# Third attention of a two-block transformer: key, value and query blocks in two halves, heads attended between blocks

## What is computed

```python
def second_block(...):
    ...
    for layer in range(DEPTH):
        mod = c_act @ ada_w[layer] + ada_b[layer]
        sh1, sc1, g1, sh2, sc2, g2 = jnp.split(mod, 6, axis=-1)
        hn = modulate_2(rms_norm_2(h, norm1_g[layer]), sh1, sc1)
        y = recurrent_mixer(hn, ...) if layer < N_A_LAYERS else chunk_attention(hn, ..., k_pad, v_pad)
        h = h + g1[:, None, :] * y
        hn = modulate_2(rms_norm_2(h, norm2_g[layer]), sh2, sc2)
        h = h + g2[:, None, :] * sqrelu_mlp(hn, mlp_w1[layer], mlp_w2[layer])
        if layer == N_A_LAYERS - 1:
            k_pad, v_pad = shared_kv(h, c_act, kv_norm_g, kv_ada_w, kv_ada_b, kv_w, k_norm_g)

def shared_kv(h, c_act, ...):
    ...
    hn = modulate_2(rms_norm_2(h, kv_norm_g), shift, scale)
    k, v = jnp.split(hn @ kv_w, 2, axis=-1)
    k = rms_norm_2(k.reshape(bsz, s, N_HEADS, HEAD_DIM), k_norm_g)      # 16 heads of 64

def chunk_attention(hn, w_q, q_norm_g, rel_bias, w_o, k_pad, v_pad):
    ...
    q = rms_norm_2((hn @ w_q).reshape(bsz, s, N_HEADS, HEAD_DIM), q_norm_g)
    sc = jnp.einsum("bqhd,bkhd->bhqk", qc, kc) * scale + bias           # relative bias, masked
    p = jax.nn.softmax(sc, axis=-1)
    return jnp.einsum("bhqk,bkhd->bqhd", p, vc) @ w_o
```

## Time and profile before

| | us |
|---|---|
| three runs of the kernel before | 1739.34, 1744.42, 1745.04 |
| their median | 1744.42 |
| the profiled execution's own time | 1744.36 |
| its span in the profile | 1742.6 |
| PE busy | 1666.6 (96%) |
| DVE busy | 1285.7 (74%) |
| ACT busy | 826.7 (47%) |
| POOL busy | 243.3 (14%) |
| granted clock of TensorE, mean | 0.99 of full speed |

### The profile page before, as it was taken

One profiled execution on the slowest core, in us unless ns is written; L12 is line 12 of the kernel. 1 busy time (PEld: TensorE's weight loads), 2 busy tenths in 40 slices (PEclk: granted clock), 3 DMA queues, 4 the chain that ended last, 5 costly groups with the idle time before them and its releaser, 6 DMA issues.

```text
span 1742.6 us, 28904 instructions
## 1 busy us (share of the span) xinstructions
PE 1666.6 (96%) x11946; PEld 1487.3 (85%) x11946; DVE 1285.7 (74%) x1777; ACT 826.7 (47%) x1196; POOL 243.3 (14%) x199
## 2 busy tenths in 40 slices
PE   6999989999999999999999999969999999899999
PEld 3897667788788876986999999959999999699999
DVE  4777863887988878857578777797998878657453
ACT  3433762543224333636554546575636444555362
POOL 0323001011001111440310121013000220030000
PEclk9999999999999999999999999989999999999999
DMA  8744002233565458320347566634998956037542
GB/s 304 276 159 169 2 1 97 97 145 115 187 241 203 175 202 311 122 73 2 122 151 272 204 202 244 217 123 172 357 364 323 335 213 240 27 125 287 187 176 73
DMA packets 46578, 317.87 MB, mean 182 GB/s; under 512 B 5232, under 2 KB 6256, under 8 KB 12272
## 3 DMA queue, kind: packets, MB, share of 16 engines
q1 hardware_dynamic: 45936, 312.68, 49.2%
q0 software_dynamic: 512, 3.35, 0.5%
HBM read 314.96 MB, written 1.05 MB: 181 GB/s over the span
## 4 chain that ended last, share of the span: by engine, by line
PE 81%; DVE 11%; ACT 3%; issue 3%; POOL 2%; DMA 1%; DVEq 0%; ACTq 0%
PE PM L1629 22%; PE PM L1630 22%; PE PM L1631 22%; PE PM L1904 2%; DVE wlo L1030 2%; PE PX L1940 1%; DVE acc L1064 1%; PE PX L1602 1%; PE PX L1813 1%; PE PO L1966 1%; PE PX L1870 1%; PE PO L1955 1%; DVE Hlo L1527 1%; PE PM L1713 1%; PE PM L1715 1%
## 5 line engine op out<-in xcount | busy, mean ns | idle before, releaser
L1629 PE MATMUL PM<-Hhi,whi 128*128 128x256 f32 (+1 forms) x1686 | 525.9, 312 | 8.6 <-DVE Hlo L1441 3.0
L1630 PE MATMUL PM<-Hlo,whi 128*128 128x256 f32 (+1 forms) x1686 | 522.1, 310 | 0.0
L1631 PE MATMUL PM<-Hhi,wlo 128*128 128x256 f32 (+1 forms) x1686 | 521.9, 310 | 0.0
L1030 DVE TENSOR_TENSOR wlo<-raw,whi 128x2048 fp32r<-128x2048 f32 (+2 forms) x199 | 438.0, 2201 | 96.7 <-ACT whi L721 96.1
L721 ACT ACTIVATE whi<-raw 128x2048 fp32r<-128x2048 f32 (+3 forms) x204 | 365.5, 1791 | 150.8 <-PE PM L1631 95.1
L1629 PEld LDWEIGHTS PM<-Hhi,whi 128*128 128x128 f32 x1686 | 322.2, 191 | 33.4 <-issue 9.7
L1631 PEld LDWEIGHTS PM<-Hhi,wlo 128*128 128x128 f32 x1686 | 322.4, 191 | 16.5
L1630 PEld LDWEIGHTS PM<-Hlo,whi 128*128 128x128 f32 x1686 | 322.4, 191 | 15.8
L1629 PE MATMUL PM<-Ghi,whi 128*128 128x256 f32 (+1 forms) x864 | 265.2, 307 | 1.7 <-DVE X L1211 1.6
L1631 PE MATMUL PM<-Ghi,wlo 128*128 128x256 f32 (+1 forms) x864 | 263.2, 305 | 0.0
L1630 PE MATMUL PM<-Glo,whi 128*128 128x256 f32 (+1 forms) x864 | 263.2, 305 | 0.0
(11 more groups left out here) (226 smaller groups left out, 2244.8 us busy)
## 6 DMA issues: line engine op xcount, KB each, us to landing
raw<-in_ada SPq DMA_DIRECT2D x104, 1024.0 KB, 4.9
raw<-in_wm SPq DMA_DIRECT2D x93, 1024.0 KB, 5.0
raw<-in_wl SPq DMA_DIRECT2D x68, 1024.0 KB, 4.9
raw<-in_wl SPq DMA_DIRECT2D x32, 704.0 KB, 4.2
raw<-in_wm SPq DMA_DIRECT2D x5, 768.0 KB, 4.4
raw<-in_wm SPq DMA_DIRECT2D x4, 704.0 KB, 4.1
X<-in_x SPq DMA_DIRECT2D x1, 2048.0 KB, 12.0
bias<-in_bias POOLq DMA_DIRECT2D x1, 2048.0 KB, 11.1
```

Source lines behind the costliest of these rows:

```text
L1030: dve.tensor_tensor(wslot(wlo, i, usize(u)), slot_raw(n, usize(u)), wslot(whi, i, usize(u)).bitcast(F32), ALU.subtract)\
L1629: pe.matmul(out, st_hi, mv_hi, start=first, stop=False)
L1630: pe.matmul(out, st_hi, mv_lo, start=False, stop=False)
L1631: return pe.matmul(out, st_lo, mv_hi, start=False, stop=last)
```

## The change

It has three parts.

**Start.** The squares of chunks 1 to 6 of the first norm are added on DVE (counter sqadd_dve), and PE sums two instead of eight. The first ada pieces to be loaded are those of direct half 2, then w0, then the others; the order of the direct work on PE, DVE and ACT follows. The warm matmuls are 8 and 2 in place of 10 and 8, the 8 ahead of a wait. ACT makes split_hi(0) before lam's exponential, and its first Hhi waits for ada_first_done(0), which DVE now does behind its second xr.

**KV and M1.** The order of units becomes k0 k1 v4 v5 q0 q1, k2 k3 v6 v7 q2 q3 (156 to 167). The step of norm 7 goes; its pieces are worked in steps 156 to 159 (query_part, query_hi, query_lo) into the second half of Hhi and Hlo. The attention's steps are ordered by head group first; steps 0 to 4 are spread over units 162 to 166 and later, the rest comes in m_late between parts of the first two out units (168, 169), whose products over k 0 to 3 need the first head group alone. Units 156 to 169 share the two halves of one PM bank, the scores have the other; so each score group waits for the add (sadd) of the group before. The evacuation's squares go to rsum, and keep_busy stands before turns 5 to 7 alone.

**Ada pieces.** The three pieces of units 160 to 162 go to 83, 86 and 89. Since pieces are numbered in order, every piece behind those takes an earlier place: rows(15) follows unit 93, its last piece (63) being at 92; the last rows (24) follow 153 and not 163.

The weights are laid out in the new order. The core of the diff:

```diff
-    for n in range(8):
-        add("k" if n < 4 else "v", "KV", n, KD, 256, 256, nt=2)
-    for n in range(4):
-        add("q", "M1", n, KD, 256, 256, nt=2)
+    for half in range(2):
+        for kind, at_ in (("k", 0), ("v", 4), ("q", 0)):
+            for n in range(at_ + 2 * half, at_ + 2 * half + 2):
+                add(kind, "M1" if kind == "q" else "KV", n, KD, 256, 256, nt=2)
...
-WARM_TURN = {("L1", "cq"): 3, ("L1", "bq0"): 3, ("M1", "q"): 4}
+WARM_TURN = {("L1", "cq"): 3, ("L1", "bq0"): 3}
...
+EARLY = {KV0 + 6 + n: n for n in range(5)}
...
-                if key == ("q", 0):
-                    prog.append(("norm", 7, "M1", 256))
...
-              *range(160, 163), *range(173, 177)]:
+              83, 86, 89, *range(173, 177)]:
...
-DIRECT_ORDER = [0, 2, 1, 3, 4, 5, 6, 7]
+DIRECT_ORDER = [2, 0, 3, 1, 4, 5, 6, 7]
...
-    order = [("ada", a) for a in ADA_FIRST[:4]] + [("w", 0)] + [("ada", a) for a in ADA_FIRST[4:]] + [("w", 1)]
+    order = [("ada", a) for a in ADA_FIRST[:2]] + [("w", 0)] + [("ada", a) for a in ADA_FIRST[2:]] + [("w", 1)]
...
         def pm(i, a, n):
-            return PM[:, i % 2, a:a + n]
+            if KV0 <= i < OUT0 + 2:
+                return PM[:, 0, i % 2 * 512 + a:i % 2 * 512 + a + n]
...
             root(0, 512)
+            split_hi(0)
             act.wait_ge(*at("prep", "lam"))
             act.activation(view(lamt[:, :], "p (l c) -> p l c", l=2)[:, :, 2:4], view(lamt[:, :], "p (l c) -> p l c", l=2)[:, :, 0:2],
                            ACT.Exp).then_inc(*tick("prepa", "lam"))
-            split_hi(0)
...
+                        if n == 0 and s == 0:
+                            act.wait_ge(*at("aux_dve", ("ada", ("first", 0))))
...
+                    n = EARLY.get(i)
+                    if n == 3:
+                        m_spread_copy(1)
+                    if n:
+                        m_turn_copy(n - 1)
                     evac(u)
+                    if KV0 <= i < KV0 + 4:
+                        query_hi(2 * (i - KV0))
+                        query_hi(2 * (i - KV0) + 1)
+                    if n == 4:
+                        m_out_hi(1)
+                    elif n is not None:
+                        m_exps(n)
...
+            def m_late(last):
+
+                m_max(4)
+                qk_copy(last)
+                m_max(5)
+                m_turn_copy(4)
+                m_max(6)
+                m_reciprocal(5)
+                m_turn_copy(5)
+                m_max(7)
+                m_turn_copy(6)
+                m_product(5)
+                m_reciprocal(7)
+                m_turn_copy(7)
+                m_out_lo(5)
+                m_product(7)
+                m_out_lo(7)
+
...
-            arow_copy(0)
+            for k in range(1, added(0)):
+                if k > 1:
+                    dve.wait_ge(*at("sqadd_dve", (0, k - 1)))
+                dve.wait_ge(*at("sq", (0, k)))
+                dve.tensor_tensor(sqslot(0, 0, 512), sqslot(0, 0, 512), sqslot(0, k, 512), ALU.add).then_inc(*tick("sqadd_dve", (0, k)))
             arow_copy(2)
+            ada_first_done(2)
...
+                        if n == 0 and s == 1:
+                            arow_copy(0)
+                            ada_first_done(0)
...
+                    if n:
+                        m_turn_copy(n - 1)
+                    if n == 3:
+                        m_product(1)
                     evac(u)
...
+            def m_scores(n):
+
+                x = MS[n]
+                t, nk, j = x["t"], x["nk"], x["h0"] // 4
+                pe.wait_ge(*at("aux_dve", ("qkT", unit_of("k", "KV", j), 1)))
+                pe.wait_ge(*at("aux_dve", ("qkT", unit_of("q", "M1", j), 1)))
+                if n:
+                    pe.wait_ge(*at("sadd", ("M1", n - 1)))
+                for e, h in enumerate(x["heads"]):
...
+            def m_late():
+
+                out_part(UNITS[OUT0], range(4))
+                m_scores(4)
+                out_part(UNITS[OUT0 + 1], range(4))
+                transposes(UNITS[OUT0 - 1])
+                m_scores(5)
+                m_turn(4, False)
+                m_scores(6)
+                m_turn(5, True)
+                m_values(4)
+                m_scores(7)
+                m_spread(5)
+                m_turn(6, True)
+                m_values(5)
+                m_turn(7, True)
+                m_values(6)
+                m_spread(7)
+                m_values(7)
...
             pe.wait_ge(*at("cstdma", 0))
+            warm(("first", 0), 8)
             pe.wait_ge(*at("prep", "sel"))
-            warm(("first", 0), 10)
-            for k in range(3):
-                sumsq(0, k, 512)
+            direct_part(2, 0)
+            direct_part(2, 1)
+            sumsq(0, 0, 512)
+            sumsq(0, 7, 512)
+            direct_columns(2)
             direct_part(0, 0)
-            for k in range(3, 5):
-                sumsq(0, k, 512)
             direct_part(0, 1)
-            for k in range(5, 7):
-                sumsq(0, k, 512)
-            direct_part(2, 0)
-            sumsq(0, 7, 512)
-            direct_part(2, 1)
             direct_columns(0)
-            direct_columns(2)
-            warm(("first", 1), 8)
+            warm(("first", 1), 2)
             late = []
...
+                    n = EARLY.get(i, 9)
+                    if n < 4:
+                        m_scores(n)
+                    if n == 3:
+                        m_spread(1)
                     for v in turned_at(i):
                         transposes(v)
+                    if 1 <= n <= 4:
+                        m_turn(n - 1, False)
+                    if 2 <= n <= 4:
+                        m_values(n - 2)
```

More of the change, by code:

```diff
@@ L154, in first_of, with unit_of @@
     return next(u["i"] for u in UNITS if u["kind"] == kind and u["st"] == st)
+def unit_of(kind, st, idx):
+    return next(u["i"] for u in UNITS if u["kind"] == kind and u["st"] == st and u["idx"] == idx)
+KV0 = first_of("k", "KV")
+OUT0 = first_of("out", "M1")
+EARLY = {KV0 + 6 + n: n for n in range(5)}
 def norm_pieces(n, W):
@@ new lines, in m_spread_copy, with m_turn_copy @@
+            def m_spread_copy(m):
+                key = ("R", "M1", MS[m]["grp"])
+                g = groups["M1", MS[m]["grp"]]
+                before = [q for q, v in groups.items() if v == g - 2 and q[0] == "M1"]
+                if before:
+                    act.wait_ge(*at("otlo", before[0]))
+                act.wait_ge(*at("aux", key))
+                act.activation(tslot(g % 2), aux(key), ACT.Copy).then_inc(*tick("aux_act", key))
+            def m_turn_copy(m):
+                key = ("T", "M1", m, 0)
+                if t_copier(MS[m], 0) != "aux_act":
+                    return
+                act.wait_ge(*at("aux", key))
+                if pt_before(m) is not None:
+                    act.wait_ge(*at("pv", ("M1", pt_before(m))))
+                act.activation(MT[m][:, 0:512], aux(key), ACT.Copy).then_inc(*tick("aux_act", key))
@@ L975, in _ @@
                 elif step[0] == "attn":
[L976 to L977 removed]
+                    if step[1] == "M1":
+                        m_late()
+                    else:
+                        attn(step[1])
                 elif step[0] == "lsplit":
@@ L1206, in residual @@
                 cs = chunks_of(u)
-                each = 256 if u["kind"] == "lpart" else 512
+                each = 256 if u["kind"] == "lpart" or OUT0 <= i < OUT0 + 2 else 512
                 for m, c in enumerate(cs):
@@ new lines, in m_turn @@
+            def m_turn(m, busy):
+                x = MS[m]
+                nc_ = x["nk"] // 128
+                pieces = [(e, c) for e in range(4) for c in range(nc_)]
+                per = len(pieces) // t_banks(x)
+                for b in range(t_banks(x)):
+                    key = ("T", "M1", m, b)
+                    dst = take(key)
+                    if busy and b == 0:
+                        keep_busy(dst)
+                    if b == 0:
+                        pe.wait_ge(*at("p", ("M1", m)))
+                    for c in range(per):
+                        ins = pe.transpose(dst[:, c * 128:c * 128 + 128], MP[m][:, m_piece(m, *pieces[b * per + c])], ident)
+                    ins.then_inc(*tick("aux", key))
@@ new lines, in m_spread @@
+            def m_spread(m):
+                key = ("R", "M1", MS[m]["grp"])
+                rec = stat(REC, groups["M1", MS[m]["grp"]])
+                dst = take(key)
+                pe.wait_ge(*at("rec", key))
+                for s in range(8):
+                    e, c = s % 2, s // 2
+                    ins = pe.matmul(dst[64 * e:64 * e + 64, c * 128:c * 128 + 128], rec[:, s:s + 1].to_broadcast([P, 64]), ident,
+                                    start=True, stop=True)
+                ins.then_inc(*tick("aux", key))
@@ L2033, in _ @@
                 if step[0] == "attn":
-                    last = UNITS[first_of("out", step[1]) - 1]
-                    if is_qk(last):
```

(6 more changed lines are left out.)

268 lines of the change are left out of this document (216 added, 52 removed).

## The result

The changed kernel is slower: 1754.67 us (median of four runs, 1751.33 to 1756.13) against 1744.26 before (four runs, 1739.34 to 1745.04), a ratio of 1.0061 with a 95% interval of 1.0049 to 1.0072. The forecast was 1741.5, between 1733 and 1748. Its sign was wrong, and the time lies 6.7 us above its range. The profiled run of the changed kernel took 1751.33 us with a span of 1749.2, 6.6 more than the span before. It is the fastest of the four, 3.3 us under their median, so its trace shows about two thirds of the 10.4 us between the medians.

A forecast was written before the change was run, and what follows sets the result against it. The prediction took PE as the bound, with 81% of the chain that ended last. Start -5.3, KV and attention -2.1, ada pieces +4.5 sum to -2.9 us: 1744.36 to 1741.5, 8-in-10 range 1733.0 to 1748.0.

The forecast's parts named there:

- Part 1: The start: fewer sums on PE bring the first unit matmul to about 31.4 instead of 36.73, a gain of 5.3 us.
- the walk: Operations followed in order through PE, DVE and ACT with traced durations: start to 31.4 us, k0 to out 137.9 us.
- the new wait: Start: ACT's first Hhi waits for arow_copy(0), direct_columns(0) and ada_first_done(0); 0.7, 0.8 and 0.3 us put down.
- Part 2: KV and attention: 5.5 us saved by filling PE's gaps, less 3.4 for lower clock, net gain 2.1 us.
- Three spells: KV and attention: lower-clock stretches after PE waits, three expected, counted as two more than before at 1.7 us each.
- these pieces were in it already, so they still fit: Units 156 to 159: norm 7's query pieces fit, as DVE is busy 48.8 and ACT 30.5 of 59 us.
- The ring: From the first scores, unit 162: DVE and ACT alternate, 10.2 to 11.1 us a step against PE's 7.4 to 9.4.
- Part 3: Ada pieces: free at 83, 86, 89; waits before rows(15) 2.6 and rows(17) 0.5, clock 1.4: loss of 4.5 us.
- R3: Attention: up to five table loads on ACT, 6.4 us, plus 1.7 for a clock spell: 1749.6 us; chance 0.12.
- R1: KV and attention: PE sets the pace in early steps, 7.2 us of waits before q3 absent: 1734.3 us; chance 0.2.
- R2: L1: rows(15) does not stall, so the 4.5 us loss shrinks to 0.5: 1737.5 us; chance 0.12.
- R4: Start: a late transfer or the wait for ada_first_done sets the first Hhi, the 5.3 gain gone: 1746.8; chance 0.1.

The follow-up runs named there:

- e2: The kernel before with only the new start; 1740.25 us, ratio 0.9980 to the kernel before.
- e9: e7 with ACT making the high part of the unit three ahead before the query pieces in units 156 to 159; 1733.20 us.
- e7: e4 with ACT making the high part of the unit three ahead before the exponentials in units 162 to 165; 1740.13 us.
- e1: The kernel before with only the ada pieces of units 160 to 162 moved to 83, 86, 89; 1753.70 us, ratio 1.0051.
- e3: The changed kernel with the ada piece of unit 92 at 93; 1751.18 us, ratio 1.0039 to the kernel before.
- e13: e1 with ACT making the high part of the unit two ahead before the gate's operation in units 83 to 91; 1753.99 us.
- e5: e4 with the old start; 1751.28 us, ratio 1.0049 to the kernel before.
- e4: The changed kernel with the three ada pieces at 102, 104, 106 instead of 83, 86, 89; 1746.84 us, ratio 1.0018 to the kernel before.
- e8: e2 with 26 warm matmuls instead of 8 ahead of the first direct half; 1738.82 us, ratio 0.9974 to the kernel before.

## Why the prediction was wrong, step by step

**Part 1, the start: mechanism right, size too large.** First unit matmul forecast at 31.4, found at 32.15; forecast gain 5.3, measured 3.5 (e2), 5.3 in the changed kernel's own profile by unit 8. Every step of the walk is in the timeline. Up to xr(1) they came 0.4 to 1.0 us sooner than walked (29.05 forecast, 28.10 found), although direct_part(2) took 1.93 for its first half and 1.81 for its second instead of 1.07. The term that was too small is the new wait: from the copy of arow to the first Hhi 1.8 us were put down, and it took 3.0 (28.12 to 31.09), as direct_columns(0) took 1.83 in place of 0.95 at the lower clock. The walk took PE's durations at the higher clock throughout; a second stretch at the lower one, 27.0 to 33.8 in the changed kernel and 29.7 to 36.5 in e2, also lies over unit 0's first matmuls. That stretches at the lower clock would fall into the start was not costed at all.

**Part 2: sign wrong.** Forecast -2.1, measured about +4.0 by difference. Two errors are in the forecast's own sum. It booked the 1.2 us of rows(24) as saved here and did not pay it in part 3, to which they only moved. And it set a walk of 137.9 without any lower clock against a measured 143.4 which holds two stretches of it, the one behind 1488 and a second:

```profile
1514.00:1516.00 2.00, 1.07 (x10) 1.10 (x12) 1.34 (x3) 1.29 (x5) 0.00 (x0) 0.73 0.00 0
1516.00:1518.00 2.00, 2.00 (x13) 1.38 (x10) 0.66 (x1) 1.78 (x6) 0.00 (x0) 0.50 0.00 0
```

Three spells expected after are then 3 x 1.7 on top of the walk, not 2 x 1.7. With both put right, the forecast's own figures give part 2 a loss of 0.8 (2.1 - 1.2 - 1.7), and the whole no change, 1744.4.

The term that failed beyond that is the one set to nothing, "these pieces were in it already, so they still fit". It read DVE's 48.8 of 59 us as slack for the query pieces. They were in those 59 us, but behind v7, and q0 began at 1456.62, 51 us after k0. Now q0 begins after four units. In the changed kernel DVE waits 1.25 to 1.99 us for whi in each of those units, since ACT's Hhi of two query pieces stands before split_hi, and PE lost 1.73 + 2.42 there, with 5.8 to 6.9 us in all hanging on that order (e9). The ring from unit 162 on was forecast with 16 us of gaps in all; apart from the 4.15 and a 0.68 the trace has 13.4. That half was right, and e7 shows its cause. But the forecast stopped at the walk and took the order as given; in the walk split_hi was the term that nobody in the same step needed, and that one exchange is worth 6.7 us. Against the 141.3 us forecast for the stretch (137.9 and 3.4 for the clock) it took 144.8, 3.5 more: gaps 2.2 more (18.2 against 16), PE's own work 3.0 more than counted (144.8 - 18.2 - 1.7 = 124.9 against 137.9 - 16 = 121.9; which item was counted short is not shown), and the clock 1.7 less, since the lower level came once.

**Part 3: mechanism right for one half, the other half missed.** The stand before rows(15) was 3.02 (2.6 forecast) and the lower clock behind it cost 3.4 in the profiled run (1.4 forecast as a mean; e1 and e3 had none, e13 had it). What failed is the first sentence, that the pieces at 83, 86 and 89 cost nothing because DVE idles 1.38 us per up unit and three units' idle time covers a piece. One unit's idle time was all that a piece got back: the split right behind it starts without idle time, the next two have their 1.38 again, and the delay stays. For the third piece, ahead of the down units, it was their 0.84. On ACT the splits run 1.4, 1.7 and 1.9 us later behind the three pieces and never catch up. From unit 90 on PE has gaps of 1.07, 0.68 and 0.97 us, the first and the last until DVE has freed its bank. Behind that come the stand before rows(15), 0.76 before rows(17) (0.5 forecast), the 1.2 of rows(24), which no part of the forecast paid, and 0.7 at M0's wait, which rows(16) no longer fills. The whole part came to 9.9 (e1) instead of 4.5.

**The rivals.** R3, the tables: five loads are in the trace as forecast, but four are under a wait: 1.0 to 2.4 us of idle time follow each of them, as the 1.01 for the maximum behind the one of 1474.44. The fifth is at 1503.36; the root starts 0.01 us behind it, and DVE's sum, which it also needs, had ended 0.5 us before. At e7, where ACT is tighter, one of the exponentials' loads shows:

```profile
1466.50 1.28 ACT L924 ACT_TABLE_LOAD   x1
1467.80 0.41 ACT L924 ACTIVATE acc<-acc,st 128x128 f32<-128x128 f32 x1
```

1.28 us and then at once the exponential. The drain of 1.4 us which the Trainium skill ("ScalarE: Activation LUTs", What ACT_TABLE_LOAD costs) adds is not seen here either. R1 (PE sets the pace before q3) describes e9 and not this kernel. R2 did not happen. Of R4, the new wait does set the first Hhi, as the walk had it, but the gain was not gone.

**The range** was built from each part's bounds, but the two terms that failed were set at nothing and had no upper bound of their own. A walk through the three engines' orders for units 156 to 160 too, as was made from 162 on, might have shown the 4.15; and three pieces at their full 2.74 would have put part 3's upper bound at 5 + 8.2.

**What stays open.** What part 2 alone costs is known to some 3 us by the medians (4.0) and lies between 2.5 and 3.9 by the traces of e5 and of the changed kernel against e1's. The number of lower-clock stretches differs from run to run (none in e9, one in e4, two in e5 between k0 and out), so a single profile does not settle a difference of 2 us. What keeps an up unit's delay from being made up is not settled: e13 ruled out the one order on ACT, and the chain through ACT and POOL and DVE's own load are left.

## What to carry to other kernels

Idle time that comes back at every unit need not add up to slack. Look at what ended it; where it is a partner engine at every unit, added work of 2.7 to 3.2 us got one idle time of 1.4 back here and was late by the rest for good. Time saved in a stage because work left it is no saving until the stage that takes the work has paid for it, and a walk at the full clock must be set against a measured stretch with its slow spells taken out. Work that moves into a shorter stretch must be summed against that stretch alone, and in an engine's order the operations nobody in the loop needs (here the split of a later unit) go first: that was worth 6.7 and 6.9 us. When a list of due places is shifted, look at each sum behind it for the place its last piece now has: one piece at an interleaved pair cost 3 us and, in two of three profiles, a spell of the lower clock; and a sum that had filled a wait left it open.

## What the runs showed of the hardware

In the changed kernel's start PE stood idle 5.15 us up to 16.21; the granted clock from 16 to 20 was 0.50, one of its two levels (1.2 GHz), and direct halves took 1.93 us in place of 1.07. Keeping PE busy over that stand gave 1.00 there, and the lower level then came at 27 to 37 us in e8, beginning in the second of three gaps of 1.19, 1.43 and 0.91 us. The stand of 3.0 us before rows(15) was followed by the lower level in the changed kernel (0.51 from 1028 to 1034) and in e13, and not in e1: the price of this gap was its length plus 0 or 3.4 us, and one profile does not tell which. Shorter idle times were followed by it too: before, PE idled 0.99 and 1.49 us, the second until 1514.93, and then had 0.50 from 1516 to 1518. A table load took 1.28 us on ACT, and where nothing else was waited for the next operation began 0.01 us behind it (1504.64 and 1504.66 in the changed kernel).
